# RWKV scan: the second lane set one step behind the first

## The reference, cut to what matters

```
def step(S, inp):
    sa = jnp.einsum('bhvk,bhk->bhv', S, -kk_t)
    S = (S * w_t[:, :, None, :] + sa[..., None] * (kk_t * a_t)[:, :, None, :]
         + v_t[..., None] * k_t[:, :, None, :])
    y = jnp.einsum('bhvk,bhk->bhv', S, inp[5]) if len(inp) == 6 else None
...
for d, rev in enumerate((False, True)):
    S_ctx, yc = _wkv_scan(S0, decay_c, k_c, vc, kkc, a_c, rc, rev)
    _, y = _wkv_scan(S_ctx, decay, k_d, v, kk, a_d, r, rev)
    wkv = wkv + y
```

## Time and profile before

| | before |
|---|---|
| median of 3 runs | 3795.48 us (3793.31 to 3803.53) |
| the profiled execution | 3804.48 us, its span 3803.2 us |
| the scan's eight head pairs | from 2614 to about 3310 us of the span |
| from one wide L to the next (ACT L3650) | 86.9 us (2730.28 to 2817.21) |
| busy share of the span (the page) | PE 93%, PEld 60%, DVE 44%, POOL 37%, ACT 31% |

### The profile page before, as it was taken

How to read it: one execution, slowest core, us unless ns; L and a number is a source line. 1 busy time by engine, 2 the same in 40 slices (tenths; PEclk the granted TensorE clock), 3 DMA queues, 4 the chain that set the end, 5 groups by cost and what they waited for, 6 DMA issues and landing times.

```text
span 3803.2 us, 72363 instructions
## 1 busy us (share of the span) xinstructions
PE 3532.9 (93%) x31740; PEld 2276.7 (60%) x31740; DVE 1675.3 (44%) x2942; ACT 1181.9 (31%) x2157; POOL 1393.0 (37%) x1239
## 2 busy tenths in 40 slices
PE   7999899999999989898999998999888888889998
PEld 3755584344554555554555554456667677658887
DVE  1245562366531234444333425524666666433344
ACT  3154342322214633413000002114666556320002
POOL 1230550133312245665323333344444444144443
PEclk9999899999999989999999999999999999999999
DMA  5441005311112135301111211331000000122221
GB/s 190 133 137 34 2 14 178 127 47 54 49 49 68 45 111 177 134 23 52 59 56 56 66 51 50 105 112 51 17 17 17 17 17 3 55 70 89 89 89 67
DMA packets 196435, 263.78 MB, mean 69 GB/s; under 512 B 6135, under 2 KB 151671, under 8 KB 194072
## 3 DMA queue, kind: packets, MB, share of 16 engines
q1 hardware_dynamic: 188960, 241.74, 19.2%
q10 hardware_dynamic: 7160, 17.41, 1.2%
HBM read 246.55 MB, written 12.58 MB: 68 GB/s over the span
## 4 chain that ended last, share of the span: by engine, by line
PE 53%; ACT 6%; DVE 4%; issue 4%; POOL 1%; DMA 0%; ACTq 0%; DVEq 0%; SPq 0%; POOLq 0%
PE ps L238 42%; PE ps L3238 2%; PE ps L771 2%; ACT mem L848 1%; PE ps L382 1%; PE ps L798 1%; PE ps L786 1%; PE ps L489 1%; DVE mem L829 1%; PE ps L3757 1%; POOL mem L3540 0%; PE ps L498 0%; PE ps L3765 0%; ACT mem L858 0%; ACT mem L3173 0%
## 5 line engine op out<-in xcount | busy, mean ns | idle before, releaser
L238 PE MATMUL ps<-mem 64*64 64x64 f32 (+4 forms) x25120 | 2624.0, 295 | 98.4 <-ACT mem L3173 26.1
L238 PEld LDWEIGHTS ps<-mem 64*64 64x64 f32 (+1 forms) x25120 | 1704.2, 150 | 1025.4 <-issue 519.6
L3103 POOL TENSOR_TENSOR mem<-mem 128x256 f32<-128x256 f32 (+1 forms) x264 | 228.2, 878 | 342.6 <-ACT mem L3650 176.8
L866 POOL TENSOR_SCALAR mem<-mem 128x768 f32<-128x768 f32 (+2 forms) x128 | 219.3, 1727 | 202.7 <-DVE mem L832 202.7
L2366 ACT ACTIVATE mem<-ps 128x384 f32<-128x384 f32 (+1 forms) x80 | 35.7, 446 | 779.1 <-PE ps L238 736.8
L2353 POOL TENSOR_TENSOR mem<-mem 128x512 f32<-128x512 f32 (+1 forms) x80 | 100.9, 1261 | 445.2 <-PE ps L238 368.4
L596 POOL TENSOR_TENSOR mem<-mem 128x512 f32<-128x512 f32 (+1 forms) x72 | 75.3, 1064 | 417.5 <-ACT mem L591 414.3
L2377 DVE TENSOR_TENSOR mem<-mem,ps 128x384 f32<-128x384 f32 (+1 forms) x80 | 39.9, 499 | 415.8 <-PE ps L238 415.8
L3238 PE MATMUL ps<-mem 128*128 128x128 f32 x960 | 166.4, 289 | 26.6 <-DVE mem L3162 14.0
L3162 DVE TENSOR_TENSOR mem<-mem,ps 128x256 f32<-128x256 f32 (+1 forms) x220 | 109.6, 514 | 110.8 <-PE ps L238 109.9
L3171 ACT ACTIVATE mem<-ps 128x256 f32<-128x256 f32 (+1 forms) x220 | 101.5, 462 | 173.3 <-PE ps L3238 173.0
(11 more groups left out here) (339 smaller groups left out, 4082.7 us busy)
## 6 DMA issues: line engine op xcount, KB each, us to landing
mem<-i_mod_w SPq DMA_DIRECT2D x48, 1024.0 KB, 6.9
mem<-i_ffn_wg SPq DMA_DIRECT2D x22, 1024.0 KB, 5.3
mem<-i_ffn_wu SPq DMA_DIRECT2D x22, 1024.0 KB, 5.3
mem<-i_e_w_in SPq DMA_DIRECT2D x16, 1024.0 KB, 6.2
mem<-i_o_w_in SPq DMA_DIRECT2D x16, 1024.0 KB, 5.4
mem<-i_ffn_wd SPq DMA_DIRECT2D x16, 1024.0 KB, 4.9
mem<-i_e_mod_w SPq DMA_DIRECT2D x12, 1024.0 KB, 11.8
mem<-i_o_mod_w SPq DMA_DIRECT2D x12, 1024.0 KB, 6.6
```

Of the source, the lines that this page charges most:

```text
L238: ins = e.h.matmul(out, l, r, start=(i == 0), stop=(i == n - 1))
L866: K.pool.h.tensor_scalar(w, w, stat(i, o, 1), None, MUL).then_inc(*nm.up(tag, i, o))
L3103: K.pool.h.tensor_tensor(m3(self.slot(l)), self.lraw, bm(C(K, f"cm{self.d}", l, 64), 2 * self.np), MUL).then_inc(*self.mk.up(key, l))
```

## The change

Lane 1's steps pass through a generator that yields once before it begins. It is done for all four engines, for every head pair. Every lane-1 step thus stands one round later in every queue, against finish, lane 0 and front, and a head pair takes 42 rounds in place of 41.

```diff
             for hp in range(9):
-                streams = (... [weave(w(hp, 0), w(hp, 1))] if hp < 8 ...) + ([self.later(f(hp + 1))] ...)
+                streams = (... [weave(w(hp, 0), self.behind(w(hp, 1)))] if hp < 8 ...) + ([self.later(f(hp + 1))] ...)
                 run(*streams)
...
+    def behind(self, lane):
+
+        yield
+        yield from lane
```

More of the change, by code:

```diff
@@ L3331, in run @@
             for hp in range(9):
-                streams = ([z(hp - 1)] if hp else []) + ([weave(w(hp, 0), w(hp, 1))] if hp < 8 else []) + ([self.later(f(hp + 1))] if hp < 7 else [])
+                streams = ([z(hp - 1)] if hp else []) + ([weave(w(hp, 0), self.behind(w(hp, 1)))] if hp < 8 else []) + ([self.later(f(hp + 1))] if hp < 7 else [])
                 run(*streams)
         self.loads()
+    def behind(self, lane):
+        yield
+        yield from lane
     def later(self, front):
```

## The result

| | before | after |
|---|---|---|
| median (lowest to highest), four runs each | 3796.27 us (3793.31 to 3803.53) | 3892.52 us (3886.75 to 3898.23) |
| ratio, 95% interval | | 1.0251, 1.0230 to 1.0272 |
| span of the profiled execution | 3803.2 us | 3890.4 us |
| from one wide L to the next, seven distances | 84.3 to 89.8 us | 94.2 to 102.2 us |

The change makes the kernel 96 us slower, 2.5%. The direction was forecast, the size was not: 3849 us with a range up to 3870. Nearly all the loss lies in the scan: 85 of the 87 us between the two profiled executions.

A forecast was written before the change was run, and what follows sets the result against it. PE, busy 87% in mid-scan, was taken as the bound. Seven wide halves (36 us), eight narrow (17) and the last wide half (1) added 54 to 3804.48, giving 3858, less 9.0 for the median: 3849.5; 8-in-10 range 3807 to 3870.

The forecast's parts named there:

- Steady level, nothing: Ordinary scan levels: PE's step order keeps the same pattern with the lanes' parts exchanged; zero gain booked.
- narrow half +2.1: Each of eight narrow halves: 0.6 us for its opening, 0 for its middle, 1.5 for its end.
- Opening of the wide half +3.7: Wide half's start: later bt 2.65 us, a change of step 0.3, first1 waiting 0.8; booked seven times.
- Levels +1.4: Wide half's levels: front's runs on DVE and ACT delay lane steps, 1.4 us in each of seven.
- End of a head pair, 0: Wide half's end: new waits at ps0 and wkv1 take in PE's instruction gaps, so nothing is lost.
- Clock, 0 to 5.6: Wait before bt may bring lower-clock stretches, 7 x 0.8 us; 0 in the sum, 5.6 for the upper end.
- The sum against the median: Whole kernel: the median of the runs taken as 9.0 us below the profiled execution, so 3858 becomes 3849.5.
- the changes between transposes and products: PE's switches between transposes and 64x64 products: 0.3 us per added group, 9.3 us where PE sets the pace.
- half: Rival: added waits fall on instruction gaps and each other, leaving bt's loss and narrow openings; 23 us, 3819; 18%.
- more: Rival: the instruction gaps stay (+21 us) and the clock falls, above +75 us; 4%.

The follow-up runs named there:

- narrow: Kernel before with lane 1 one step behind lane 0 in the narrow half alone, both lanes together in the wide half; 3822.0 us, ratio 1.0058.
- earlylag: Kernel before with lane 1 one step behind in the wide half's opening alone, from L to lv; 3831.4 us, ratio 1.0082.
- fill2: Kernel after with 8, 4 and 4 unread PE products ahead of lane 0's bt, third-level B and ps in wide halves; 3874.4 us, ratio 1.0197.
- front17: Kernel after with the front started one round later on all engines; 3845.4 us, ratio 1.0113.
- fill: Kernel after with 12, 6 and 7 unread PE products ahead of lane 0's bt, third-level B and ps in wide halves; 3895.0 us, ratio 1.0248.

## Why the prediction was right in direction and wrong in size

- **Steady level, nothing; narrow half +2.1.** The size is right, in part by luck: the mean narrow half is 1.5 us longer, and eight of them cost 22 us with their clock in *narrow* where 17 were booked. At its end ps of both lanes waits 0.8 and 1.0 us for DVE's negation where 0.9 and 1.1 were worked out. But the middle, booked at 0, has the wait of 2.01 us ahead of a B in seven narrow halves (the longest wait for that copy was 0.9 before). The normalisation's own wait for ACT fell only from 6.4 to 2.7 us in all; what makes up for the rest no run isolates.
- **Opening of the wide half +3.7.** Right: bt at 10.59 after L for 10.65, its wait 3.73 for 3.6, *first* of lane 1 waits 0.69 for 0.8. *earlylag*, which has no wait for the mask, gives 30 us with the clock in it: 7 x 2.9 = 20 booked, and 24 us more at the lower level.
- **Levels +1.4.** The places were right: A of the third level comes 4.85 behind that of the second for 5.25, and B 8.49 for 8.8, waiting 1.89. The size too, without the clock: from lane 1's first A to its fifth (by ACT's copies T, mean of seven head pairs) it is 20.6 us before, 22.9 after, and 21.6 in *fill2*, which has no low clock there.
- **End of a head pair, 0.** This step failed too, by some 9 us of standing. The waits came as worked out, 2.06 for 2.4 and 1.38 for 1.5, and the instruction gaps did mostly fall into them: the time in which PE waits for nothing that the trace shows went from 17.8 to 2.9 us in seven head pairs. But the new waits are longer than the gaps that they took in. The sum had the two equal.
- **Clock, 0 to 5.6.** This is the step that failed most. I took one stretch per head pair from the earlier trace rows, at 0.8 us, behind bt alone, and then left it out of the sum. Twenty more came in seven head pairs, most behind the new waits of 1.9 us and more and two at the last one of 1.38, and a piece of work with one in it was 1.1 to 1.5 us longer. The time at the lower level rose by 68 us; at the 0.36 to 0.47 us that the pads gave back for each, that is 25 to 32 us; PE's busy time rose by 32.7. I had worked out the waits of 3.6 and 2.4 myself and had not asked of the second what I asked of the first.
- **The sum against the median.** I took 9 us off for the distance of the profiled execution from the median. Fifteen other executions of the kernel before went from 3791 to 3805, so this was scatter. For the kernel after the two are within 1 us (3891.7 and 3892.5), so the 9 were not to be taken off a second kernel.

Profile against profile the account closes without the medians. The table has seven head pairs in three parts, marked by ACT's copies of L and of lane 1's fifth T. One B of lane 0 (4 us in seven) stands behind the fifth A before and ahead of it after. "Low" is the time at the lower level after; before, 6.8 us of it stood in the third part.

| part, us | before | after | PE stands before | after | low | booked |
|---|---|---|---|---|---|---|
| wide L to lane 1's fifth A | 254.8 | 314.6 | 26.4 | 60.4 | 44.4 | 36 |
| from there to the narrow L | 106.7 | 121.3 | 20.5 | 29.1 | 23.9 | 0 |
| narrow L to wide L | 247.0 | 257.8 | 30.6 | 40.5 | 6.8 | 15 |

Standing grew by 34, 9 and 10 us, 52 in all, where 7 x 7.2 = 50 were booked. So the total of the waits was right with two errors that cancel in part, +9 at the end and -5 in the narrow half. The other 33 of the 85 us are longer busy time, for which the sum had nothing; the changes between transposes and products (0.3 us a group by the prediction's line) are in it as well and no run parts them from the clock. Against the forecast of 3849 the 9 us of the median come on top.

The forecast did not see that half of the loss hangs on where the front stands: it worked out the front's ACT and DVE runs at two places as fixed costs of the lag, when moving the front by the same round removes most of them: in *front17* PE stands 32.6 us in the first part of the table and 20.5 in the second, 6 and 0 more than before; the 42.7 in the third remain. The rival *half* (gaps and waits fall on each other) is refuted, and *more* (gaps stay, clock falls) is what came, in its number and for the clock; its gaps did not stay.

A gap of 1.98 us with no releaser also stands inside the dense products of *fill2*. By the Trainium skill ("Runtime: NRT & Kernel Launch", Instruction fetch mechanics) crossing a block of 256 instructions is mostly hidden. If this gap and the one of the earlier trace rows are such crossings, they disagree with the page; no run shows that they are, and the same products in *fill* have none.

## What to carry to other kernels

When one of several interleaved streams is shifted, everything that was placed against it has to move as well, in all engines together: shifting the front in one engine gave nothing or a loss, in all of them half of the loss back. Price each new wait of TensorE twice, for its length and for the slower work that follows it, and ask this of every new wait, not of the longest alone: here waits of 1.9 to 3.7 us were mostly followed by slower work, waits of 1.4 seldom. A wait removed from one queue is gained only if the next queue in the chain is early as well; two runs here took a wait of 1.5 and of 3.7 us away and gained nothing and less than half.

## What the runs showed that I had not expected

- Small products that nobody reads, put into a wait, made the whole kernel faster, 1.0113 to 1.0078 of the kernel before, by holding the granted clock at 0.99 in place of 0.95.
- What the lower clock costs can't be read from its ratio alone: the same 320 records took 7.89 us at a mean clock of 0.78, and at full clock 6.39 without a gap in *fill* and 8.81 with one in *fill2*. Over a head pair 1 us less at the lower level gave back 0.36 to 0.47 us.
- In the narrow half the lag made a wait of 2.01 us for ACT's copy behind the normalisation's products, seven times, as much in all as the 1.89 of the third level. No term of the sum had it.
- A pad of 128x256 took 0.41 us in *fill*, so 12 of them were 5.0 us, longer than the wait they were to fill, and took back all that the clock gave.
